# A router's choice by pairwise comparison, two remainders put behind the selection, and one norm's order

## The chip, the cores and the metric

The kernel runs on one core of a Trainium2 chip. The metric is the device time of one execution in microseconds, the median of the runs. A core has five engines that run side by side and meet only at semaphores: TensorE (PE, with PEld for its weight loads), VectorE (DVE), ScalarE (ACT), GpSimd (POOL) and SyncE (SP, which issues most DMAs here).

## The reference, cut to what matters

One inference step of a two-layer decoder over 336 tokens (16 meta tokens, 256 of a prompt, 64 of samples), model width 1024. Layer 0 is RWKV-7 time mixing, layer 1 differential attention; behind each stands the same kind of mixture of 16 experts with a shared router. The change lies in this mixture:

```python
def _moe(x, router_w, router_b, w_gate, w_up, w_down):
    s = jax.nn.sigmoid((xt @ router_w).astype(f32))
    sel = s + router_b.astype(f32)
    grp = lax.top_k(sel.reshape(-1, N_GROUPS, EXPERTS_PER_GROUP), 2)[0].sum(-1)
    _, gidx = lax.top_k(grp, TOPK_GROUPS)                 # 1 of 4 groups
    gmask = jax.nn.one_hot(gidx, N_GROUPS, dtype=f32).sum(1)
    emask = jnp.repeat(gmask, EXPERTS_PER_GROUP, axis=-1) > 0
    _, eidx = lax.top_k(jnp.where(emask, sel, -jnp.inf), TOP_K)   # 2 of its 4 experts
    wts = jnp.take_along_axis(s, eidx, -1)
    wts = wts / wts.sum(-1, keepdims=True)
    gates = ...                                           # wts at the chosen experts
    for e in range(N_EXPERTS):
        h = jax.nn.silu(xt @ w_gate[e]) * (xt @ w_up[e])
        y = y + gates[:, e:e + 1] * (h @ w_down[e])
```

Ahead of it the residual is normalized (`_layernorm(alpha*x + h)`). Ties go to the lower index, as in `top_k`.

## The kernel before

The 336 tokens stand as three tiles of 128, 128 and 80 rows (`TOK`; tile 2 is the one of 80). All instructions are written out by hand, engine by engine, in the order in which they run; each engine works through its own list and waits on semaphores. `experts(l, n0)` is written once per engine and called for each of the two layers. Its routing part runs thus:

- **Norm.** DVE adds the residual out of PSUM and sums each row (`residual`, lines 2187 and 2176), ACT makes the squares and the root (`spread_of`), DVE takes the reciprocal (2195) and scales (2202, `normalize`). PE turns the tile (`turn`, 1253), ACT and DVE copy the turned halves out, PE makes the logits, and ACT the sigmoid. Meanwhile ACT keeps a rounded copy of each normalized tile (`xtm_hi`, `normed_copy`), and what the rounding left, `xtm_lo`, is a subtraction: by POOL for tile 0 and by DVE (`remainder`, 2292) for tiles 2 and 1.
- **Choice.** DVE adds the bias (2334), takes the six pair sums of each group and their maximum (2338, 2340), and then `first_best` three times: maximum, equal, times a weight that falls with the index, maximum, equal. Once it is for the group, twice for the experts within the masked group. A `dve.drain()` stands between steps that depend on each other. The running counts over the tiles follow (2373 to 2376).
- **Rank.** PE multiplies the choice by a triangle of ones and adds the counts: each token's place in its expert's list (semaphore `rt_pe`). Meanwhile DVE makes the weights of the chosen experts (2377 to 2387). Then DVE adds the rank (2391) and `select` (2239) writes the 0/1 matrix that puts tokens in the 64 slots of each expert.
- **Gather.** PE multiplies the parts `xtm_hi`, `xtm_lo` of the three tiles by that matrix, four passes `i` of 12 matmuls. Passes 0 and 2 use PSUM bank 0, passes 1 and 3 bank 1. ACT empties bank 0 and DVE bank 1 (`gathered`, 2245); passes 2 and 3 wait for that. With all four emptied, the expert pairs begin (`pair`): gate, up, down, two experts at a time, eight pairs.

The experts' weights stream through a ring of slots; SP issues the next load when PE has freed a slot (`free`). So the first pair's gate matmuls also start the stream of the later weights.

Of the kernel before, what the change touches and what calls it, by code (L numbers as in the profile page):

```python
# [8 lines left out]
ALU = mybir.AluOpType  # L9
ACT = mybir.ActivationFunctionType  # L10
AX = mybir.AxisListType.X
# [5 lines left out]
P = 128  # L17
# [22 lines left out]
QUAD = 4 * SLOTS  # L40
TURNS = [(0, 1), (2, 3), (4, 5), (6,), (7,)]
ROWS = [0, 1, 0, 1, 0, 1, 0, 0]
ALPHA = 4.0 ** 0.25
# [45 lines left out]
def constants():  # L89
# [26 lines left out]
    parts["iota"] = np.tile(np.arange(CAP), (P, 1))  # L116
    parts["w16"] = np.tile(np.arange(E_, 0, -1), (P, 1))
    parts["w4"] = np.tile(np.arange(G_, 0, -1), (P, 1))
    parts["valid"] = np.concatenate([p < n for _, n in TOK], 1)
    parts["caus"] = np.where(q > p, -BIG, 0.0)  # L120
# [19 lines left out]
def build(nc, I, O, const, at):  # L140
    ctx = ExitStack()
    with ctx:
        sems = {}

        def S(name):
            name = SHARED.get(name, (name, 0))[0]
            if name not in sems:
                sems[name] = ctx.enter_context(nc.semaphore(name))
            return sems[name]
# [589 lines left out]
        def _(pe):  # L739
# [368 lines left out]

            def gather(q, i):

                for h, t in ((0, 0), (0, 1), (0, 2), (1, 0), (1, 2), (1, 1)):
                    t0, k = TOK[t]
                    if q % 4 == 0 and i == 0 and h and t:
                        pe.wait_ge(S("xtm_lo"), 2 * (q // 4) + (1 if t == 2 else 2))
                    for c in (2 * i, 2 * i + 1):
                        o = QUAD * (c % 2)
                        m = mm(ps[:, i % 2, o:o + QUAD], XTM[h][t][0:k, P * c:P * c + P],
                               SelF[q % 2][0:k, t].rearrange("p e s -> p (e s)"), h == t == 0 and c == 2 * i, h == t == 1 and c == 2 * i + 1)
                m.then_inc(S("xg_mm"), 1)

# [52 lines left out]
            def pair(l, n0, j):  # L1173
# [16 lines left out]
                def more_rows():  # L1190
                    if j < PAIRS - 2:
                        pe.wait_ge(S("sel_ready"), q + 2)
                        for i in (2 * (j % 2), 2 * (j % 2) + 1):
                            pe.wait_ge(S(("xga_ready", "xgb_ready")[i % 2]), 2 * (q + 1) + i // 2)
                            gather(q + 1, i)

# [49 lines left out]
            def experts(l, n0):  # L1246
# [44 lines left out]
                pe.wait_ge(S("sel_ready"), 4 * l + 1)  # L1291
                for i in range(4):
                    if i >= 2:
                        pe.wait_ge(S(("xga_ready", "xgb_ready")[i % 2]), 8 * l + i // 2)
                    gather(4 * l, i)
                for j in range(PAIRS):
# [184 lines left out]
        def _(act):  # L1481
# [245 lines left out]
            def experts(l, n0):  # L1727
                if l == 0:
                    act.wait_ge(S("in_lora"), 16 * 7)
                spread_of(2 * l, 0)  # L1730
                spread_of(2 * l, 1)
                turned_copy(l, 0)
                spread_of(2 * l, 2)
                normed_copy(l, 0)
                turned_copy(l, 1)
                turned_copy(l, 2)
                act.wait_ge(S("rt_pe"), 5 * l + 4)
                act.wait_ge(S("rt_dve"), 6 * l + 1)
                f(rt[0][:, 0:32], ps[:, 6, 0:32], ACT.Sigmoid)
                f(rt[0][0:TOK[2][1], 32:48], ps[0:TOK[2][1], 6, 32:48], ACT.Sigmoid).then_inc(S("s_ready"), 1)  # L1740
                normed_copy(l, 1)
                normed_copy(l, 2)
                for i in (0, 2):
                    gathered(4 * l, i)
                for j in range(PAIRS):
                    if j == PAIRS - 1:
                        act.wait_ge(S("route_ready"), l + 1)
                        overflow(act, l, "act", lambda i, b, n: more_block(l, n), lambda: None, lambda: None)
                    pair(l, j)
# [143 lines left out]
        def _(dve):  # L1893
# [386 lines left out]
            def experts(l, n0):  # L2280
# [30 lines left out]
                residual(l, 0)  # L2311
                residual(l, 1)
                normalize(2 * l, 0)
                residual(l, 2)
                normalize(2 * l, 1)
# [14 lines left out]

                score, sel, a1, a2, oh, msk0, msk, _ = rt
                gm, ga, gb, gc = gs
                m12 = ga[:, 0:12]
                tt(v3(sel), v3(score), rbB.unsqueeze(1).to_broadcast([P, 3, E_]), ALU.add)
                dve.drain()

                for d, o, k in ((1, 0, 3), (2, 3, 2), (3, 5, 1)):
# [3 lines left out]
                dve.drain()  # L2341
                top1 = cntf[:, 0:3]

                def first_best(dst, val, tmp, width, weight):

                    dve.tensor_reduce(top1, v3(val), AX, ALU.max)
                    dve.drain()
                    tt(v3(tmp), v3(val), top1.unsqueeze(2).to_broadcast([P, 3, width]), ALU.is_equal)
                    dve.drain()
                    tt(v3(tmp), v3(tmp), weight.unsqueeze(1).to_broadcast([P, 3, width]), ALU.mult)  # L2350
                    dve.drain()
                    dve.tensor_reduce(top1, v3(tmp), AX, ALU.max)
                    dve.drain()
                    tt(v3(dst), top1.unsqueeze(2).to_broadcast([P, 3, width]),
                       weight.unsqueeze(1).to_broadcast([P, 3, width]), ALU.is_equal)
                    dve.drain()

                first_best(gb, gm, ga, G_, mc("w4"))
                gmask = gb.unsqueeze(2).to_broadcast([P, 12, 4])
                tsc(gc, gb, BIG, -BIG, ALU.mult, ALU.add)  # L2360
                tt(g12(a1), g12(sel), gmask, ALU.mult)
                dve.drain()
                tt(g12(a1), g12(a1), gc.unsqueeze(2).to_broadcast([P, 12, 4]), ALU.add)
                dve.drain()
                first_best(msk0, a1, a2, E_, mc("w16"))
                stt(a1, msk0, -2 * BIG, a1, ALU.mult, ALU.add)
                dve.drain()
                first_best(oh, a1, a2, E_, mc("w16"))
                tt(msk, msk0, oh, ALU.add)
                dve.drain()  # L2370
                tt(v3(msk), v3(msk), mc("valid").unsqueeze(2).to_broadcast([P, 3, E_]), ALU.mult)
                dve.drain()
# [14 lines left out]
                tsc(a2, msk, -1e6, 1e6, ALU.mult, ALU.add)  # L2387
                remainder(2)
                dve.wait_ge(S("rt_pe"), 5 * l + 5)
                dve.drain()  # L2390
                tt(rank3.rearrange("p t n -> p (t n)"), a2, ps[:, 7, 0:48], ALU.add)
                dve.drain()
                select(4 * l)
                dve.tensor_reduce(cntp[:, 0:1], ps[:, 7, 64:80], AX, ALU.max)
                cp(cnt_i[0:1, 0:E_], ps[0:1, 7, 64:80])
                dve.drain()
                cp(cnt_i[0:1, E_:E_ + 1], cntp[0:1, 0:1])
                dve.drain().then_inc(S("route_ready"), 1)
                remainder(1)
                dve.wait_ge(S("route_ready"), l + 1)  # L2400
# [182 lines left out]
```

## Time and profile before

| | |
|---|---|
| runs shown | 1216.82, 1219.72, 1220.41 us, median 1219.72 us |
| profiled execution, its own time | 1218.88 us |
| its span | 1217.2 us |
| busy share of the span | PE 89%, DVE 44%, ACT 29%, POOL 6% |
| chain that ended last, by engine | PE 74%, DVE 12%, DMA 6%, ACT 3%, issue 2% |
| TensorE clock, mean granted | 0.937 of 2.4 GHz |
| DMA | 274 MB, 225 GB/s on average |

The busy shares are averages over stages that differ. The routing of a layer is a short stage between two long ones: PE is idle for parts of it, and the weight stream too. A stage's own rows tell what a change there is worth. The profiled execution lies inside the range of the runs, 0.84 us under their median, so its rows can be set against either.

### The profile page before, as it was taken

Reading aid. Unit: us, or ns where it says so; the run is one execution under the profiler, and the core shown is the slowest. Engines: PE = TensorE matmul, PEld = TensorE weight load, DVE = VectorE, ACT = ScalarE, POOL = GpSimd, SP = SyncE. Lnnn points to the kernel's source line nnn. Section 1 sums busy time; section 2 is a strip of 40 time slices with the busy share of each in tenths; the row PEclk is TensorE's granted clock in tenths of the full one; section 3 lists DMA queues with packets and bytes.
Section 4 is the critical chain, followed back from the end, with each engine's and each line's share of the span. In section 5 each row is a group of like instructions: output and inputs, shape, how many; then the busy total and the mean of one; then the engine's idle time right before and its main releaser. Section 6 shows DMA issues by size and latency. Waiting matters only on the chain.

```text
span 1217.2 us, 23537 instructions
## 1 busy us (share of the span) xinstructions
PE 1081.1 (89%) x10193; PEld 760.0 (62%) x10194; DVE 541.1 (44%) x1068; ACT 358.0 (29%) x720; POOL 70.0 (6%) x101
## 2 busy tenths in 40 slices
PE   4989989899888869999998799999879599999984
PEld 3877978899855644555443699976636444444532
DVE  5856536556566571212122754474444631222215
ACT  3435424443232421111111533473232411111102
POOL 2002100011000000000000112011100000000000
PEclk8989979999997979999999899999989699999997
DMA  9503010011041929999999803464733289999991
GB/s 333 215 10 69 19 47 3 3 38 38 25 154 70 396 95 421 422 422 423 422 423 398 316 1 125 159 234 144 290 139 140 106 348 422 423 423 423 422 401 48
DMA packets 58251, 274.16 MB, mean 225 GB/s; under 512 B 5169, under 2 KB 5690, under 8 KB 34082
## 3 DMA queue, kind: packets, MB, share of 16 engines
q1 hardware_dynamic: 48160, 237.58, 48.6%
q0 software_dynamic: 9360, 34.72, 8.8%
q8 instruction: 83, 1.36, 0.5%
q10 hardware_dynamic: 626, 0.32, 0.1%
q14 instruction: 22, 0.18, 0.0%
HBM read 266.18 MB, written 6.46 MB: 224 GB/s over the span
## 4 chain that ended last, share of the span: by engine, by line
PE 74%; DVE 12%; DMA 6%; ACT 3%; issue 2%; DVEq 1%; SPq 0%; POOLq 0%; ACTq 0%; POOL 0%
PE ps L742 69%; DMA arena<-in_moe_w_up 5%; ACT arena L1484 2%; PE ps L883 1%; PE ps L1373 1%; DVE arena L1924 1%; DMA arena<-in_cache_k 1%; ACT arena L1487 1%; PE ps L1089 1%; PE ps L1205 1%; DVE pwr_lo L1930 0%; PE ps L1253 0%; DVE arena L2024 0%; DMA arena<-in_x_prompt 0%; DVE arena L2483 0%
## 5 line engine op out<-in xcount | busy, mean ns | idle before, releaser
L742 PE MATMUL ps<-arena 64*64 64x64 f32 (+10 forms) x7348 | 625.8, 323 | 61.8 <-DVE arena L2376 15.6
L742 PEld LDWEIGHTS ps<-arena 64*64 64x64 f32 (+4 forms) x7348 | 355.5, 140 | 309.1 <-issue 220.7
L1487 ACT COPY arena<-ps 128x512 f32<-128x512 f32 (+7 forms) x294 | 121.4, 432 | 338.8 <-PE ps L742 182.2
L2267 DVE TENSOR_TENSOR arena<-arena,ps 128x512 f32<-128x512 f32 x16 | 17.4, 1085 | 185.5 <-PE ps L742 185.5
L1484 ACT ACTIVATE arena<-ps,arena 128x256 f32<-128x256 f32 (+5 forms) x96 | 45.5, 507 | 133.5 <-PE ps L742 102.4
L2278 DVE SCALAR_TENSOR_TENSOR yy_lo<-ps,arena,yy_hi 128x512 fp32r<-128x512 f32 x32 | 22.7, 747 | 123.0 <-ACT yy_hi L1484 123.0
L1484 ACT ACTIVATE pw_hi<-arena 128x1024 fp32r<-128x1024 f32 x40 | 42.0, 1057 | 89.0 <-PE ps L742 82.8
L742 PE MATMUL ps<-px_hi,pw_hi 128*128 128x336 f32 x192 | 63.4, 330 | 1.4 <-DVE px_lo L2157 1.0
L742 PE MATMUL ps<-px_lo,pw_hi 128*128 128x336 f32 x192 | 61.9, 322 | 0.0
L742 PE MATMUL ps<-px_hi,pw_lo 128*128 128x336 f32 x192 | 61.8, 322 | 0.0
L1484 ACT ACTIVATE yy_hi<-ps,arena 128x512 fp32r<-128x512 f32 x32 | 20.5, 684 | 106.3 <-PE ps L742 106.3
L1484 ACT ACTIVATE arena<-arena 128x1024 f32<-128x1024 f32 (+9 forms) x73 | 42.9, 629 | 26.9 <-DVE arena L2176 20.6
L2146 DVE TENSOR_TENSOR pw_lo<-arena,pw_hi 128x1024 fp32r<-128x1024 f32 x24 | 29.4, 1225 | 43.2 <-ACT pw_hi L1484 43.1
L742 PE MATMUL ps<-rx_hi_hi,pwr_hi 128*128 128x336 f32 x96 | 34.3, 357 | 12.6 <-ACT rx_hi_hi L1484 8.0
L742 PE MATMUL ps<-yy_hi,sg 128*128 128x512 f32 (+1 forms) x96 | 40.4, 421 | 4.8 <-DVE arena L2256 2.7
L1930 DVE TENSOR_TENSOR pwr_lo<-arena,pwr_hi 128x1024 fp32r<-128x1024 f32 x24 | 29.4, 1223 | 33.8 <-ACT pwr_hi L1484 33.6
L742 PE MATMUL ps<-pw_hi,px_hi 128*128 128x512 f32 (+1 forms) x96 | 40.7, 424 | 4.1 <-ACT pw_hi L1484 3.8
L1484 ACT ACTIVATE arena<-ps 128x512 f32<-128x512 f32 (+4 forms) x23 | 11.4, 506 | 103.9 <-PE ps L742 103.8
L742 PE MATMUL ps<-pw_hi,px_lo 128*128 128x512 f32 (+1 forms) x96 | 39.6, 413 | 0.0
L742 PE MATMUL ps<-pw_lo,px_hi 128*128 128x512 f32 (+1 forms) x96 | 39.3, 409 | 0.0
L742 PEld LDWEIGHTS ps<-px_hi,pw_hi 128*128 128x128 f32 x192 | 37.1, 193 | 1.9 <-issue 1.9
L742 PE MATMUL ps<-yy_lo,sg 128*128 128x512 f32 (+1 forms) x96 | 37.8, 394 | 0.0
(229 smaller groups left out, 1387.3 us busy)
## 6 DMA issues: line engine op xcount, KB each, us to landing
arena<-in_moe_w_gate SPq DMA_DIRECT2D x64, 1024.0 KB, 15.7
arena<-in_moe_w_up SPq DMA_DIRECT2D x64, 1024.0 KB, 18.8
arena<-in_moe_w_down SPq DMA_DIRECT2D x64, 1024.0 KB, 17.0
arena<-in_rwkv_w_rkv SPq DMA_DIRECT2D x6, 2048.0 KB, 19.5
arena<-in_w_kv_shared SPq DMA_DIRECT2D x4, 2048.0 KB, 19.8
arena<-in_cache_k POOLq DMA_DIRECT2D x16, 512.0 KB, 4.6
arena<-in_cache_v POOLq DMA_DIRECT2D x16, 512.0 KB, 6.8
arena<-in_rwkv_w_out SPq DMA_DIRECT2D x2, 2048.0 KB, 10.3
```

What stands on the lines that cost most here:

```text
L742: return pe.matmul(out, lhsT, rhs, start=start, stop=stop)
L883: m = pe.transpose(ps[:, b + hf, P * c:P * c + P], src[:, 4 * hf + c, o0:o0 + P], ident)
L1089: m = pe.transpose(ps[0:n, 4 + g % 4, P * c:P * c + P], X[:, 4 * hf + c, t0:t0 + n], ident)
L1205: m = pe.transpose(ps[:, 2, P * f:P * f + P], HH[:, P * f:P * f + P], ident)
L1373: m = pe.transpose(ps[:, 2 * g + hf, P * c:P * c + P], PGK[b % 4][:, g, P * (4 * hf + c):P * (4 * hf + c) + P], ident)
L1484: return act.activation(out, in_, func, **k)
L1487: return act.copy(out, in_)
L1924: stt(X[:, c, :], sgT[:, c, :], mixv[m][:, c:c + 1], xT[:, c, :], ALU.mult, ALU.add).then_inc(S("mix_ready"), 1)
L1930: tt(lo, w_in(L_RKV + n // 4)[:, :, P * (n % 4):P * (n % 4) + P], hi.bitcast(F32), ALU.subtract).then_inc(S("rw_lo"), 1)
L2146: tt(lo, w_in(L_KV + co // 4)[:, :, P * (co % 4):P * (co % 4) + P], hi.bitcast(F32), ALU.subtract).then_inc(S("pw_lo"), 1)
L2267: tt(HH.rearrange("p (k q) -> p q k", k=NF), HS.rearrange("p (q k) -> p q k", k=NF), bank(3).rearrange("p (q k) -> p q k", k=NF), ALU.mult ...
L2278: stt(YY[ROWS[j]][1][:, h], bank(4 + hf), gsl, YY[ROWS[j]][0][:, h].bitcast(F32), ALU.mult, ALU.subtract).then_inc(S("yl_ready"), 1)
```

## The change

It has three parts, each made in both layers.

1. **The choice.** `first_best` goes. A new function `ahead(val)` takes three tiles of four values, compares every value of a four with every other (`is_gt` and `is_ge`, 48 elements each), puts the `is_ge` result where the other stands first in order (a copy with a mask), and adds up how many stand ahead of each. A group is chosen where nobody stands ahead of it; the four values of the chosen group are summed out of the 16, and `ahead` is run on them. Chosen are those with fewer than 1.5 ahead; rows without a token have the bound -1. Three constants of 23 columns give way to two of 19.
2. **The remainders of tiles 2 and 1** come behind `select`; the counts that `route_ready` announces come behind them. PE's gather is cut to match: passes 0 and 1 first do the parts that need neither remainder, then both do tile 2's, then both tile 1's.
3. **The norm.** `residual` of tile 2 stands ahead of `normalize` of tile 0 on DVE, and ACT makes tile 2's spread ahead of its copy of the turned tile 0.

```diff
+PARTS = [(0, 0), (0, 1), (0, 2), (1, 0), (1, 2), (1, 1)]
-    parts["w16"] = np.tile(np.arange(E_, 0, -1), (P, 1))
-    parts["w4"] = np.tile(np.arange(G_, 0, -1), (P, 1))
-    parts["valid"] = np.concatenate([p < n for _, n in TOK], 1)
+    parts["first"] = np.tile((np.arange(4)[None, :] < np.arange(4)[:, None]).reshape(1, 16), (P, 1))
+    parts["below"] = np.concatenate([np.where(p < n, 1.5, -1.0) for _, n in TOK], 1)
...
-                for i in range(4):
-                    if i >= 2:
-                        pe.wait_ge(S(("xga_ready", "xgb_ready")[i % 2]), 8 * l + i // 2)
-                    gather(4 * l, i)
+                for i in range(2):
+                    gather(4 * l, i, PARTS[0:4])
+                pe.wait_ge(S("xtm_lo"), 2 * l + 1)
+                for i in range(2):
+                    gather(4 * l, i, PARTS[4:5])
+                pe.wait_ge(S("xtm_lo"), 2 * l + 2)
+                for i in range(2):
+                    gather(4 * l, i, PARTS[5:6])
+                for i in range(2, 4):
+                    pe.wait_ge(S(("xga_ready", "xgb_ready")[i % 2]), 8 * l + i // 2)
+                    gather(4 * l, i, PARTS)
...
-                turned_copy(l, 0)
                 spread_of(2 * l, 2)
+                turned_copy(l, 0)
...
-                normalize(2 * l, 0)
                 residual(l, 2)
+                normalize(2 * l, 0)
...
+                def ahead(val):
+                    other = v3(val).unsqueeze(2).to_broadcast([P, 3, 4, 4])
+                    own = v3(val).unsqueeze(3).to_broadcast([P, 3, 4, 4])
+                    tt(g44(r4), other, own, ALU.is_gt)
+                    tt(g44(g4), other, own, ALU.is_ge)
+                    dve.drain()
+                    dve.copy_predicated(v3(r4), mc("first").bitcast(U32).unsqueeze(1).to_broadcast([P, 3, 16]), v3(g4))
+                    dve.drain()
+                    dve.tensor_reduce(ga, g12(r4), AX, ALU.add)
+                    dve.drain()
...
+                ahead(gm)
+                tsc(gb, ga, 0.5, None, ALU.is_lt)
+                dve.drain()
+                tt(g12(a1), g12(sel), gb.unsqueeze(2).to_broadcast([P, 12, 4]), ALU.mult)
+                dve.drain()
+                dve.tensor_reduce(v3(gm), a1.rearrange("p (t g n) -> p t n g", t=3, g=4), AX, ALU.add)
+                dve.drain()
+                ahead(gm)
+                tt(v3(gc), v3(ga), mc("below").unsqueeze(2).to_broadcast([P, 3, 4]), ALU.is_lt)
+                dve.drain()
+                tt(g44(msk), v3(gb).unsqueeze(3).to_broadcast([P, 3, 4, 4]), v3(gc).unsqueeze(2).to_broadcast([P, 3, 4, 4]), ALU.mult)
...
-                remainder(2)
                 dve.wait_ge(S("rt_pe"), 5 * l + 5)
                 ...
                 select(4 * l)
+                remainder(2)
+                remainder(1)
                 ...
                 dve.drain().then_inc(S("route_ready"), 1)
-                remainder(1)
```

On DVE, at the first layer's norm: L2187 and L2176 are `residual`, L2195 and L2202 `normalize`, L2285 the copy of a turned tile. Before, from the reciprocal of tile 0 on:

```order
L2195 RECIPROCAL arena<-arena 128x1 [waits ln_sd]
L2202 TENSOR_SCALAR arena<-arena 128x1024
L2187 SCALAR_TENSOR_TENSOR arena<-arena,ps 80x512 [waits tile_mm]
L2187 SCALAR_TENSOR_TENSOR arena<-arena,ps 80x512
L2176 TENSOR_SCALAR arena<-arena 80x1
L2195 RECIPROCAL arena<-arena 128x1 [waits ln_sd]
L2202 TENSOR_SCALAR arena<-arena 128x1024
L2285 COPY arena<-ps 128x4x128 [waits nt_mm]
```

After, with the same lines six further down (L2193, L2182, L2201, L2208, L2291), from the residual of tile 2 on:

```order
L2193 SCALAR_TENSOR_TENSOR arena<-arena,ps 80x512 [waits tile_mm]
L2193 SCALAR_TENSOR_TENSOR arena<-arena,ps 80x512
L2182 TENSOR_SCALAR arena<-arena 80x1
L2201 RECIPROCAL arena<-arena 128x1 [waits ln_sd]
L2208 TENSOR_SCALAR arena<-arena 128x1024
L2201 RECIPROCAL arena<-arena 128x1 [waits ln_sd]
L2208 TENSOR_SCALAR arena<-arena 128x1024
L2291 COPY arena<-ps 128x4x128 [waits nt_mm]
```

The 80-row residual has moved ahead of the 128-row tile's reciprocal and scaling; the rest keeps its order.

On DVE, from the last step of the weights on: L2391 adds the rank, L2239 is `select`, `xtm_lo_55` and `xtm_lo_54` are the remainders of tiles 2 and 1, L2394 to L2397 the counts, L2245 empties the gather's bank. Before:

```order
L2387 TENSOR_SCALAR arena<-arena 128x48
L2292 TENSOR_TENSOR xtm_lo_55<-arena,xtm_hi_52 80x128x8 [waits xtm_hi]
L2391 TENSOR_TENSOR arena<-arena,ps 128x48 [waits rt_pe]
L2239 TENSOR_TENSOR sel_56<-arena 128x768
L2394 TENSOR_REDUCE arena<-ps 128x1
L2395 CAST cnt_i<-ps 1x16
L2397 CAST cnt_i<-arena 1x1
L2292 TENSOR_TENSOR xtm_lo_54<-arena,xtm_hi_51 128x128x8 [waits xtm_hi]
L2245 TENSOR_SCALAR arena<-ps,arena 128x256 [waits xg_mm,route_ready]
```

After (rank L2392, `select` L2245, remainders L2298, counts L2397 to L2400, emptying L2251):

```order
L2389 TENSOR_SCALAR arena<-arena 128x48
L2392 TENSOR_TENSOR arena<-arena,ps 128x48 [waits rt_pe]
L2245 TENSOR_TENSOR sel_56<-arena 128x768
L2298 TENSOR_TENSOR xtm_lo_55<-arena,xtm_hi_52 80x128x8 [waits xtm_hi]
L2298 TENSOR_TENSOR xtm_lo_54<-arena,xtm_hi_51 128x128x8 [waits xtm_hi]
L2397 TENSOR_REDUCE arena<-ps 128x1
L2398 CAST cnt_i<-ps 1x16
L2400 CAST cnt_i<-arena 1x1
L2251 TENSOR_SCALAR arena<-ps,arena 128x256 [waits xg_mm,route_ready]
```

Both remainders now stand between `select` and the counts, and the wait for `rt_pe` follows straight on the last step of the weights.

On PE, in the second layer's gather (`xtm_hi0`, `xtm_lo0` and so on are the parts of tiles 0 to 2), from the first pass's fourth part on. Before:

```order
L742 MATMUL ps<-sel0_56,xtm_lo0_53 128x256 x2
L742 MATMUL ps<-sel0_56,xtm_lo2_55 128x256 [waits xtm_lo]
L742 MATMUL ps<-sel0_56,xtm_lo2_55 128x256
L742 MATMUL ps<-sel0_56,xtm_lo1_54 128x256 [waits xtm_lo]
L742 MATMUL ps<-sel0_56,xtm_lo1_54 128x256
L742 MATMUL ps<-sel0_56,xtm_hi0_50 128x256 x2
L742 MATMUL ps<-sel0_56,xtm_hi1_51 128x256 x2
L742 MATMUL ps<-sel0_56,xtm_hi2_52 128x256 x2
L742 MATMUL ps<-sel0_56,xtm_lo0_53 128x256 x2
L742 MATMUL ps<-sel0_56,xtm_lo2_55 128x256 x2
L742 MATMUL ps<-sel0_56,xtm_lo1_54 128x256 x2
L742 MATMUL ps<-sel0_56,xtm_hi0_50 128x256 [waits xga_ready]
```

After:

```order
L742 MATMUL ps<-sel0_56,xtm_lo0_53 128x256 x2
L742 MATMUL ps<-sel0_56,xtm_hi0_50 128x256 x2
L742 MATMUL ps<-sel0_56,xtm_hi1_51 128x256 x2
L742 MATMUL ps<-sel0_56,xtm_hi2_52 128x256 x2
L742 MATMUL ps<-sel0_56,xtm_lo0_53 128x256 x2
L742 MATMUL ps<-sel0_56,xtm_lo2_55 128x256 [waits xtm_lo]
L742 MATMUL ps<-sel0_56,xtm_lo2_55 128x256 x3
L742 MATMUL ps<-sel0_56,xtm_lo1_54 128x256 [waits xtm_lo]
L742 MATMUL ps<-sel0_56,xtm_lo1_54 128x256 x3
L742 MATMUL ps<-sel0_56,xtm_hi0_50 128x256 [waits xga_ready]
```

The four matmuls of pass 0 that use the DVE's remainders have moved behind eight of pass 1, and each remainder is now used by both passes in a row; the wait for `xga_ready` (bank 0 emptied) opens pass 2 as before, but fewer matmuls now stand between it and the end of pass 0.

## Rows read from the trace of the kernel before

**Rows 1.** the page: part 4 by line, and one group of part 5
```profile
PE ps L742 69%; DMA arena<-in_moe_w_up 5%; ACT arena L1484 2%; PE ps L883 1%; PE ps L1373 1%; DVE arena L1924 1%; DMA arena<-in_cache_k 1%; ACT arena L1487 1%; PE ps L1089 1%; PE ps L1205 1%; DVE pwr_lo L1930 0%; PE ps L1253 0%; DVE arena L2024 0%; DMA arena<-in_x_prompt 0%; DVE arena L2483 0%
...
L742 PE MATMUL ps<-arena 64*64 64x64 f32 (+10 forms) x7348 | 625.8, 323 | 61.8 <-DVE arena L2376 15.6
```

**Rows 2.** chain of waits, whole program: start us, length us, what
```profile
620.89 29.45 DMA arena<-in_moe_w_up
```

**Rows 3.** windows: stretch, us, busy by engine, PEclk, DMA share, GB/s
```profile
418.00:420.00 2.00, 0.97 (x5) 0.97 (x6) 1.52 (x5) 1.59 (x4) 0.00 (x0) 0.69 1.00 418
430.00:432.00 2.00, 0.00 (x0) 0.00 (x0) 1.45 (x7) 0.00 (x0) 0.00 (x0) 0.50 0.08 33
...
442.00:443.00 1.00, 1.00 (x8) 1.00 (x7) 0.00 (x0) 0.17 (x1) 0.00 (x0) 0.67 0.00 0
```

**Rows 4.** timeline of DVE, first norm: start us, us, line, operation, [idle before]
```profile
415.47 0.16 DVE L2195 RECIPROCAL arena<-arena 128x1 f32<-128x1 f32 x1 [0.23 <-ACT arena L1484]
...
416.44 0.68 DVE L2187 SCALAR_TENSOR_TENSOR arena<-arena,ps 80x512 f32<-80x512 f32 x1
...
417.94 0.15 DVE L2195 RECIPROCAL arena<-arena 128x1 f32<-128x1 f32 x1
```

**Rows 5.** timeline of PE, first routing
```profile
416.58 1.10 PE L1253 MATMUL ps<-arena 128*128 128x128 f32 x8 [1.82 <-DVE arena L2202]
419.03 1.97 PE L1253 MATMUL ps<-arena 128*128 128x128 f32 x8 [1.36 <-DVE arena L2202]
...
433.44 1.46 PE L742 MATMUL ps<-arena 128*128 128x48 f32 x6 [7.79 <-DVE arena L2376]
437.94 1.62 PE L742 MATMUL ps<-sel,xtm_hi 128*128 128x256 f32 x6 [3.04 <-DVE sel L2239]
...
440.91 1.48 PE L742 MATMUL ps<-sel,xtm_hi 128*128 128x256 f32 x6
442.19 1.10 PE L742 MATMUL ps<-sel,xtm_lo 128*128 128x256 f32 x6
443.12 0.88 PE L742 MATMUL ps<-sel,xtm_hi 128*128 128x256 f32 x6
443.84 0.88 PE L742 MATMUL ps<-sel,xtm_lo 128*128 128x256 f32 x6
...
447.30 13.96 PE L742 MATMUL ps<-arena 128*64 128x512 f32 x64 [1.14 <-issue]
```

**Rows 6.** timeline of DVE, choice and selection
```profile
427.02 0.17 DVE L2346 TENSOR_REDUCE arena<-arena 128x3 f32<-128x12 f32 x1
...
428.58 0.17 DVE L2360 TENSOR_SCALAR arena<-arena 128x12 f32<-128x12 f32 x1 [0.41 <-issue]
...
432.60 0.21 DVE L2371 TENSOR_TENSOR arena<-arena 128x48 f32<-128x48 f32 x1
432.88 0.17 DVE L2373 COPY arena<-arena 128x16 f32<-128x16 f32 x1
...
434.35 0.21 DVE L2385 TENSOR_TENSOR arena<-arena 128x48 f32<-128x48 f32 x1
434.48 0.18 DVE L2387 TENSOR_SCALAR arena<-arena 128x48 f32<-128x48 f32 x1
434.57 1.89 DVE L2292 TENSOR_TENSOR xtm_lo<-arena,xtm_hi 80x1024 fp32r<-80x1024 f32 x1
436.56 0.20 DVE L2391 TENSOR_TENSOR arena<-arena,ps 128x48 f32<-128x48 f32 x1
436.84 0.96 DVE L2239 TENSOR_TENSOR sel<-arena 128x768 fp32r<-128x768 f32 x1
...
438.29 1.97 DVE L2292 TENSOR_TENSOR xtm_lo<-arena,xtm_hi 128x1024 fp32r<-128x1024 f32 x1
```

**Rows 7.** timeline of ACT, first gathered copy
```profile
441.15 1.02 ACT L1484 ACTIVATE arena<-ps,arena 128x256 f32<-128x256 f32 x2 [11.63 <-PE ps L742]
```

**Rows 8.** instructions of L2054: ns min/median/max
```profile
L2054 DVE COPY_PREDICATED arena<-arena,ps x50: 429/436/449, 175.5 to 329.7; 128x256 f32<-128x256 uint32 x50
```

More of the change, by code:

```diff
@@ L1107, in key_value_query, with gather @@
                         rows_of(co - 8)
-            def gather(q, i):
-                for h, t in ((0, 0), (0, 1), (0, 2), (1, 0), (1, 2), (1, 1)):
+            def gather(q, i, order):
+                for h, t in order:
                     t0, k = TOK[t]
-                    if q % 4 == 0 and i == 0 and h and t:
-                        pe.wait_ge(S("xtm_lo"), 2 * (q // 4) + (1 if t == 2 else 2))
                     for c in (2 * i, 2 * i + 1):
@@ L1118, in gather @@
                                SelF[q % 2][0:k, t].rearrange("p e s -> p (e s)"), h == t == 0 and c == 2 * i, h == t == 1 and c == 2 * i + 1)
-                m.then_inc(S("xg_mm"), 1)
+                if order[-1] == (1, 1):
+                    m.then_inc(S("xg_mm"), 1)
             def more_block(n0, n):
@@ L1194, in more_rows @@
                             pe.wait_ge(S(("xga_ready", "xgb_ready")[i % 2]), 2 * (q + 1) + i // 2)
-                            gather(q + 1, i)
+                            gather(q + 1, i, PARTS)
                 if j == PAIRS - 1:
@@ L1731, in experts @@
                 spread_of(2 * l, 1)
+                spread_of(2 * l, 2)
                 turned_copy(l, 0)
-                spread_of(2 * l, 2)
                 normed_copy(l, 0)
@@ L2312, in experts @@
                 residual(l, 1)
+                residual(l, 2)
                 normalize(2 * l, 0)
-                residual(l, 2)
                 normalize(2 * l, 1)
@@ L2329, in g12, with g44 @@
                     return x.rearrange("p (g n) -> p g n", n=4)
-                score, sel, a1, a2, oh, msk0, msk, _ = rt
+                def g44(x):
+                    return x.rearrange("p (t i j) -> p t i j", t=3, i=4)
+                score, sel, a1, a2, r4, g4, msk, _ = rt
                 gm, ga, gb, gc = gs
-                m12 = ga[:, 0:12]
+                top1 = cntf[:, 0:3]
+                def ahead(val):
[8 more added lines that the diff above has]
+                    dve.drain()
                 tt(v3(sel), v3(score), rbB.unsqueeze(1).to_broadcast([P, 3, E_]), ALU.add)
@@ L2341, in experts @@
                 dve.drain()
[L2342 to L2361, printed above, removed]
+                ahead(gm)
+                tsc(gb, ga, 0.5, None, ALU.is_lt)
                 dve.drain()
-                tt(g12(a1), g12(a1), gc.unsqueeze(2).to_broadcast([P, 12, 4]), ALU.add)
+                tt(g12(a1), g12(sel), gb.unsqueeze(2).to_broadcast([P, 12, 4]), ALU.mult)
                 dve.drain()
-                first_best(msk0, a1, a2, E_, mc("w16"))
-                stt(a1, msk0, -2 * BIG, a1, ALU.mult, ALU.add)
+                dve.tensor_reduce(v3(gm), a1.rearrange("p (t g n) -> p t n g", t=3, g=4), AX, ALU.add)
                 dve.drain()
-                first_best(oh, a1, a2, E_, mc("w16"))
-                tt(msk, msk0, oh, ALU.add)
+                ahead(gm)
+                tt(v3(gc), v3(ga), mc("below").unsqueeze(2).to_broadcast([P, 3, 4]), ALU.is_lt)
                 dve.drain()
-                tt(v3(msk), v3(msk), mc("valid").unsqueeze(2).to_broadcast([P, 3, E_]), ALU.mult)
+                tt(g44(msk), v3(gb).unsqueeze(3).to_broadcast([P, 3, 4, 4]), v3(gc).unsqueeze(2).to_broadcast([P, 3, 4, 4]), ALU.mult)
                 dve.drain()
```

## The prediction

> **What bounds the kernel now.** I read the chain of waits first. PE carries most of it, and one transfer stands out: the up weights of the last expert pair, 29.45 us [rows 2], and since all such waits make 5% of the 1217.2 us span, some 61 us, there is one like it in each layer [rows 1]. So the end of an expert stage hangs on its weight stream. The stream, though, is idle before: its share is 0.08 in the two microseconds from 430 [rows 3], while DVE makes the choice. It goes on when the first pair's matmuls, from 447.30 on [rows 5], free slots. What the routing saves therefore moves PE's first gate matmul, the stream and the stage's end alike, unless something fails to move along; nothing in these rows is tied to a fixed time.
>
> Then I read the routing on the engines' timelines. PE idles 7.79 us until the choice is made (DVE L2376), again 3.04 us until the selection [rows 5]. The page gives 15.6 us for the first of these waits in both layers together, twice the 7.79 [rows 1]: the second layer repeats the first, so I work out one layer and double it.
>
> **Part 1, the choice.** What goes lies between the group's maximum at 427.02 and the copy at 432.88 [rows 6]: 5.86 us, all of it on the path, since PE waits. In it 0.34 us is a hole: 0.41 idle before L2360 [rows 6], where drained steps leave about 0.07 (0.28 from start to start, 0.21 long, as between 432.60 and 432.88).
> What comes: `ahead` is four instructions on 48 or 12 elements. Two comparisons stand without a drain between, and such a pair starts 0.13 apart (434.35, 434.48) [rows 6]. The second, the masked copy and the sum are drained: 0.28 each. That is 0.97 us, twice 1.94. Five further drained steps (group mask, product, sum over groups, comparison with the bound, product) at 0.28 make 1.40. In all 3.34, and 3.68 with a hole, which I keep because its cause isn't visible. Saved: 5.86 - 3.68 = 2.18 us.
> Not shown at this size is the masked copy. The nearest row, 128x256, has a median of 0.436 us [rows 8]; 48 elements can't need more. Nor less than the 0.17 us of a 12-element step. With 0.07 of drain the price lies between 0.24 and 0.51; I take the 0.28 of a 48-element step, because the operand has that size, and keep -0.08 to +0.46 for the two.
> [...]
>
> **Part 2, the remainders.** Before, DVE's remainder of tile 2 (1.89 us) stands between the weights and the rank; the rank starts at 436.56 [rows 6]. PE has finished the rank's matmuls at 433.44 + 1.46 = 434.90 [rows 5]. Without the remainder the wait for `rt_pe` decides: 434.90 and the 0.10 that lie between the remainder's end (436.46) and the rank, 435.00. Saved: 1.56 us. Behind the waiting instruction stand `select` and both remainders, all later than the PE result anyway.
> The price is paid in the gather. Call its start G; it stays 1.38 us behind the rank (437.94 - 436.56). The remainders now start with the 0.87 us that select holds DVE (436.84 to 437.71, from 0.96 long less an overlap of 0.09, as at 434.48) and end at about G + 1.7 and G + 3.6. PE's pace in the gather is 1.28/6 = 0.213 us per matmul (440.91 to 442.19), later 0.72/6 = 0.12 (443.12 to 443.84) [rows 5]; in between the granted clock goes from the lower level (1.2 GHz) to the upper one (0.67 is the mean of that microsecond) [rows 3], about 4.7 us after G. At the slow pace PE needs tile 2's remainder after 16 matmuls, at G + 3.5, and tile 1's after 20, at G + 4.4: both are ready, the second by 0.8 us.
> But pass 0 now ends with its 22nd matmul instead of its 12th: 22 x 0.213 and 0.14 for the start (1.42 us of the first six less 1.28) give G + 4.83. Only then can ACT empty bank 0: it starts 0.24 after PE's next matmul would (441.15 against 440.91) and takes 1.02 [rows 7], and PE goes on some 0.1 later (the gap between two engines seen at the rank): pass 2 starts at G + 6.19. Before it started at 443.12, G + 5.18; ACT's work lay beside pass 1, and that cover is gone but for two matmuls. Passes 2 and 3 and their emptying are as before. Cost: 1.01 us.
> Bounds: if the level rises early, the gather waits for the remainder of tile 1 instead, two matmuls and the same 1.36 follow, G + 5.0: -0.2. If it rises only after pass 3, 24 matmuls lose 0.093 each: +2.2 on top, 3.2 in all.
>
> **Part 3, the norm.** The residual of tile 2 takes 1.50 us from its first row to the next reciprocal (416.44 to 417.94), so tile 0's reciprocal goes from 415.47 [rows 4] to about 416.66, 1.19 later, for PE's work that produced the residuals is done by then. The first turn on PE, at 416.58 before, starts at 417.77 and with its 1.10 us ends at 418.87 [rows 5]. Tile 1's normalize is ready by about 418.73 and no longer queued behind the residual; the second turn can thus start at 418.87 instead of 419.03. From there PE works without a gap through the logits, so this is the path: -0.16 us. ACT's reordered spread is done when the turned tile 0 arrives, and tile 2's turn is queued behind other PE work anyway. The bound upward: the granted clock fell during the idle time before 419.03 (0.69 in 418 to 420 [rows 3]), and the second turn took 1.97 us where the first took 1.10. If the first falls under the lower level too, it ends at 419.74: +0.71.
>
> **Sum.** -2.18 - 1.56 - 0.16 + 1.01 = -2.89 us a layer, -5.8 us in all. From the profiled execution's own 1218.88 us that gives 1213.1; the median of the runs is 0.84 higher, and for it I forecast **1213.9 us**, 0.5% less. A measurement of this kernel can tell about 0.3%, 3.7 us, from no change (the runs before lie 3.6 us apart).
> All lower bounds together: -2.18 - 0.34 (no hole) - 0.08 - 1.56 - 0.30 - 0.2, the 0.30 being the norm if the second turn starts as soon as tile 1 is ready; -4.7 a layer, 1210.4. All upper ones: -2.18 + 0.46 + 0.34 (a second hole) - 1.56 + 0.71 + 3.2 = +1.0 a layer, 1221.7; these would have to meet, in both layers.
>
> **Rivals**, each from the median.
> *The clock rises early in the gather.* The rank's matmuls now end only 1.5 us before G (434.90 to 436.38 in the old times), where it was 3.04. For it: PE is busier ahead of the gather. Against: idle until the rank is PE's state as before, and before the change PE worked 4.7 us at the lower level. The gather then costs -0.2 instead of 1.01: -4.1 a layer, 1211.5 us.
> *The lower level takes back what the routing saves.* The first turn at the lower level costs 0.87 more than forecast, passes 2 and 3 at it 2.2: together 3.1 against the 2.89 saved, and 1220.1 us. With the gather alone, 1218.3; with the first turn alone, 1215.7. For it: both stages do lie near a change of level [rows 3]. Against: in the gather the level rose before pass 2 although PE came out of idleness.
> *The new hold in the gather makes it slower than before.* PE stands still for 0.9 us (G + 5.26 to G + 6.19) between pass 1 and pass 2. If the clock then falls back at the start of pass 2 and comes back only behind the first 4.7 us of the gate matmuls, passes 2 and 3 lose 2.2 us and the gate matmuls 2.35: -2.89 + 4.55 = +1.7 a layer, 1223.0, and with the upper bound of the masked copy 1224.0. It decides once the fallen clock costs more than the 2.89 us saved. For it: after 1.36 us of idle before 419.03 the second turn ran slow. Against: before 447.30 PE idled 1.14 us [rows 5], and the gate matmuls ran 13.96/64 = 0.218 us for 512 columns, the pace of 0.12 for 256 and not of 0.213.
> The Trainium skill's page "TensorE: Matmul & The Clock Gate", section "A second HAM failure mode: psum-queue depth-cycling", says that a PE idling briefly between groups of matmuls as it cycles through PSUM banks can swing between the levels and lose throughput; this hold is of that kind. The row at 447.30 does not bear it out for one gap.
>
> **How the numbers follow.** The forecast has 0.62, the early clock 0.14, the lower level 0.20 (a quarter of it the first turn alone, still faster by over 0.3%), the slower case 0.04. Faster by over 0.3% (under 1216.1): 0.62 + 0.14 + 0.05 = 0.81, less 0.03 for the spread of the medians, 0.78. Slower by over 0.3% (above 1223.4): 0.04. Within: 0.18. The range runs from 1209.8 (the lower bounds and the spread of the runs) to 1218.0 (just under the lower level in the gather alone).
>
> **What would show it.** Right: PE's wait before L2378 shrinks from 7.79 to about 5.6 us, the one before the gather from 3.04 to about 1.5, a new PE wait of 0.9 us for ACT stands before pass 2, the first gate matmul comes 2.9 us earlier in relation to the end of the output projection, the transfer wait stays at 29 us. Wrong: a masked copy well over 0.28 us, a wait for `xtm_lo` in the gather, a longer first turn, or a transfer wait that grows by what the routing saves.

## The result, and the profile after

The changed kernel took 1210.53 us in the median of six runs, 0.9939 of the kernel before (95% interval 0.9915 to 0.9962). The six runs of before that belong to it have a median of 1216.74 us, 6.2 us more. Timed again beside 30 runs of before (median 1219.47) it was 1211.21 us in 11 runs, ratio 0.9936 (0.9912 to 0.9960): 7.8 us less, between 4.9 and 10.7. Forecast were 5.8 us less and 1213.9 us. The direction was right and the difference lies inside this interval, but the forecast time was some 3 us too high.

The profiled execution has a span of 1205.3 us, 11.9 less than before's. Not all of it is the change's. The table takes a routing apart. A routing here is the stretch from DVE's first residual row to PE's first gate matmul, cut at the starts of rows: norm and logits up to the bias, choice up to the last running count, rank up to the row that adds it, selection up to the first gather matmul, and gather.

| us | norm | choice | rank | selection | gather | sum |
|---|---|---|---|---|---|---|
| before, layer 0 | 13.85 | 7.22 | 3.35 | 1.38 | 9.36 | 35.16 |
| after, layer 0 | 13.66 | 5.02 | 1.80 | 1.38 | 10.43 | 32.29 |
| forecast of the difference | -0.16 | -2.18 | -1.56 | 0 | +1.01 | -2.89 |
| before, layer 1 | 13.94 | 7.20 | 3.34 | 1.38 | 9.44 | 35.30 |
| after, layer 1 | 12.58 | 4.67 | 1.86 | 1.38 | 10.14 | 30.63 |

Layer 0 gave 2.87 us and layer 1 4.67, 7.5 together. The other 4.4 lie in stages with the same code. The first residual row, for instance, stood at 412.14 before and at 409.49 after; in the runs below it came between 406.97 and 412.96, as it chanced.

PE's timeline after, first layer and then second, answers to [rows 5]:

```profile
415.10 2.93 PE L1252 MATMUL ps<-arena 128*128 128x128 f32 x16 [2.99 <-DVE arena L2208]
...
428.40 1.46 PE L742 MATMUL ps<-arena 128*128 128x48 f32 x6 [5.58 <-DVE arena L2378]
431.35 1.62 PE L742 MATMUL ps<-sel,xtm_hi 128*128 128x256 f32 x6 [1.49 <-DVE sel L2245]
...
434.48 2.28 PE L742 MATMUL ps<-sel,xtm_lo 128*128 128x256 f32 x10
437.50 0.98 PE L742 MATMUL ps<-sel,xtm_hi 128*128 128x256 f32 x6 [0.74 <-ACT arena L1490]
...
441.78 4.51 PE L742 MATMUL ps<-arena 128*64 128x512 f32 x20 [1.14 <-issue]
...
936.23 2.06 PE L1252 MATMUL ps<-arena 128*128 128x128 f32 x16 [2.91 <-DVE arena L2208]
```

The wait for the choice is 5.58 us where it was 7.79, the one for the selection 1.49 where it was 3.04, and the hold for ACT is there, 0.74 (0.88 in the second layer). Pass 2 starts 6.15 us behind the gather's start in layer 0, where 6.19 was forecast, and 5.87 in layer 1. The two turns run in one piece now: 2.93 us in layer 0, 2.06 in layer 1. Before, the two layers did not differ here. These are layer 1's turns before, to be set beside 1.10 and 1.97 in layer 0 [rows 5]:

```profile
941.88 1.09 PE L1253 MATMUL ps<-arena 128*128 128x128 f32 x8 [1.69 <-DVE arena L2202]
944.34 1.94 PE L1253 MATMUL ps<-arena 128*128 128x128 f32 x8 [1.37 <-DVE arena L2202]
```

DVE's timeline after, first layer and one row of the second, answers to [rows 6]:

```profile
424.19 0.21 DVE L2348 TENSOR_TENSOR arena<-arena 128x48 f32<-128x48 f32 x1
424.32 0.20 DVE L2349 TENSOR_TENSOR arena<-arena 128x48 f32<-128x48 f32 x1
424.59 0.22 DVE L2351 COPY_PREDICATED arena<-arena 128x48 f32<-128x48 uint32 x1
424.88 0.20 DVE L2353 TENSOR_REDUCE arena<-arena 128x12 f32<-128x48 f32 x1
425.16 0.17 DVE L2364 TENSOR_SCALAR arena<-arena 128x12 f32<-128x12 f32 x1
425.76 0.21 DVE L2366 TENSOR_TENSOR arena<-arena 128x48 f32<-128x48 f32 x1 [0.43 <-issue]
...
429.97 0.20 DVE L2392 TENSOR_TENSOR arena<-arena,ps 128x48 f32<-128x48 f32 x1 [0.35 <-PE ps L742]
430.25 0.96 DVE L2245 TENSOR_TENSOR sel<-arena 128x768 fp32r<-128x768 f32 x1
431.12 3.83 DVE L2298 TENSOR_TENSOR xtm_lo<-arena,xtm_hi 80x1024 fp32r<-80x1024 f32 x2
...
949.09 0.18 DVE L2385 RECIPROCAL arena<-arena 128x3 f32<-128x3 f32 x1 [0.41 <-issue]
```

The masked copy takes 0.22 us, 0.29 to the next start, where 0.28 was taken. The undrained pair starts 0.13 apart. The hole (0.43 us in which DVE waits for nothing that the profile shows) is still in the choice of layer 0. In layer 1 it has slid to the weights of the experts, where the wait for PE's rank hides nearly all of it. The remainders end 3.6 us behind the gather's start.

The chain of waits after, answering to [rows 2]: the transfer wait is still there in both layers, about as long as before (29.45 and 29.02 us). It starts 173.3 and 173.1 us behind the first gate matmul, where it was 173.6 and 173.8. So the stream did move along with that matmul.

```profile
615.06 29.86 DMA arena<-in_moe_w_up
...
1134.39 29.57 DMA arena<-in_moe_w_up
```

### The profile page after: what moved, and what is told of

It is laid out like the page before. It is cut to its first block, busy times and chain, and to the rows that moved or that the text cites. A ratio compares the mean times of both kernels' runs of the same rounds, so it can differ in the third digit from the quotient of the medians.

```text
span 1205.3 us, 23503 instructions
## 1 busy us (share of the span) xinstructions
PE 1076.9 (89%) x10193; PEld 755.7 (63%) x10194; DVE 537.3 (45%) x1052; ACT 358.0 (30%) x720; POOL 70.1 (6%) x101
## 3 DMA queue, kind: packets, MB, share of 16 engines
q8 instruction: 83, 1.36, 0.5%
## 4 chain that ended last, share of the span: by engine, by line
PE 75%; DVE 11%; DMA 6%; ACT 3%; issue 2%; DVEq 1%; SPq 0%; POOLq 0%; ACTq 0%; POOL 0%
PE ps L742 69%; DMA arena<-in_moe_w_up 5%; ACT arena L1490 1%; PE ps L883 1%; PE ps L1379 1%; DVE arena L1930 1%; DMA arena<-in_cache_k 1%; ACT arena L1493 1%; DVE arena L2193 1%; PE ps L1089 1%; PE ps L1204 1%; DVE pwr_lo L1936 0%; DMA arena<-in_x_prompt 0%; DVE arena L2030 0%; PE ps L760 0%
```

## The experiments

The theories A and B, or A and a rival, stand with each run. Each ratio is to the kernel before, timed beside it, with its 95% interval behind it. Lengths are those of the table's columns, layer 0 and layer 1, from one profiled execution of each kernel. "The level" is that of TensorE's granted clock: 1.00 in a window's column PEclk is the upper level (2.4 GHz), 0.50 the lower one (1.2 GHz). Where a text says when the level rose or fell, that is an estimate from the mean of the window in which it did.

**The changed kernel again.** 

> The changed kernel itself, timed again beside the one before. In the profiled execution the two routings (first residual row on DVE to the first gate matmul) went from 35.16 and 35.30 us to 32.29 and 30.63: -7.5 us together; the other 4.4 of the span's 11.9 us lie in stages that the change leaves alone. Theory A (the terms of the sum hold, and only TensorE's level moves a routing by a us or so): the median difference is between -5 and -8 us, and the stages left alone differ in both directions from run to run. Theory B (the change also shortens other stages): about -10 us or more, and the stretch from the start to the first residual is again 2.6 us shorter than before.

Measured: 0.9936, as above. Routings 32.23 and 30.46 us, norm 13.61 and 12.54, all as in the first profile. The 7.8 us lie in A's range, though the interval (4.9 to 10.7) reaches B's. The first residual row stood at 408.44, 3.7 us earlier than before, which is B's sign. But in the next run, with the same code in front, it stood at 412.82. So that stretch varies from profile to profile, and A is the better supported.

**Part 1 alone** (`first_best` replaced by `ahead`, nothing else). 

> Part 1 alone. Theory A: bias to running counts goes from 7.2 us to 4.7-5.0 in each layer and everything behind keeps its length: 32.8 us per routing, about -4.7 us in all. Theory B (a gather that starts earlier meets another level of the clock, as it chances): the choice is as short, but the gather changes by up to 1 us either way, -3 to -7 us.

Measured: 0.9939 (0.9914 to 0.9964), 1212.51 us. Choice 5.03 and 4.68; the routings 32.40 and 32.49, 5.6 us less together, because the gather also fell, to 8.80 and 8.85. In layer 1 the hole has moved into the rank here (3.68 us for 3.34), where nothing hides it. PE's timeline, second layer:

```profile
959.93 1.74 PE L741 MATMUL ps<-sel,xtm_lo 128*128 128x256 f32 x6
961.47 1.19 PE L741 MATMUL ps<-sel,xtm_hi 128*128 128x256 f32 x6
962.49 0.88 PE L741 MATMUL ps<-sel,xtm_lo 128*128 128x256 f32 x6
```

The pace of 0.12 us is there from 962.49 on, with pass 1's second half; before, it held from pass 2 on [rows 5]. So B is right on the gather here: the same gather, started 2.2 us earlier in its routing, met the upper level sooner, some 3.6 us behind its start where before it was 4.7 in layer 0 and 4.9 in layer 1.

**Part 2 alone.** 

> Part 2 alone. Theory A: counts to rank from 3.35 us to 1.8, gather (first matmul to first gate) from 9.4 us to 10.1-10.4 by the hold before pass 2: -0.5 to -0.9 us per routing, -1 to -2 us in all, not to be told from none by the time alone. Rival: the hold is covered and the whole 1.55 us is kept, -3 us.

Measured: 0.9991 (0.9969 to 1.0012): not to be told from none. Rank 1.81 and 1.80, hold 0.87 in both, gather 9.71 and 9.65: 1.2 to 1.3 us less per layer behind the choice. That lies between A and the rival: the hold came, as A said, but the gather grew by only 0.35 and 0.21 us, because the level rose some 3.3 and 3.2 us behind its start. But layer 0's norm took 16.08 us in the profile, 2.2 more than before, in code that this part leaves alone. PE's timeline and two windows there:

```profile
419.90 3.60 PE L743 MATMUL ps<-arena 128*32 128x128 f32 x40
423.86 0.72 PE L743 MATMUL ps<-arena 128*80 128x16 f32 x4 [0.36 <-DVE arena L2305]
```
```profile
420.00:422.00 2.00, 2.00 (x21) 1.58 (x22) 0.78 (x2) 1.20 (x1) 1.51 (x1) 0.50 1.01 410
422.00:424.00 2.00, 1.64 (x21) 1.31 (x22) 0.24 (x1) 0.00 (x0) 0.00 (x0) 0.50 1.00 422
```

The logits ran at the lower level (0.50), 3.60 us where the other profiles, and layer 1 of this one, have 2.09. That a norm can lose 2 us to the level without an edit to its code is in none of the forecast's terms. Whether this is chance or belongs to this kernel, one profile can't tell.

**Part 3 alone.** 

> Part 3 alone. First residual row to bias: 13.85 us and 13.94 before, 13.66 and 12.58 with the change. Theory A (the order of the norm gives 0.2 us; the other 1.2 in the second layer came from TensorE standing at its upper level during the turns, which differs from run to run): 13.7 in a layer where the turns run at the lower level and 12.6 where they run at the upper one, without a fixed place. Rival B (the new order itself gives 1.2 us in the second layer, where the data stand otherwise): 13.7 and 12.6 again. In all -0.3 us by A at the lower level, -1.4 by B.

Measured: 0.9982 (0.9963 to 1.0), norm 13.67 and 12.58; turns of 2.85 and 2.06 us:

```profile
418.57 2.85 PE L1253 MATMUL ps<-arena 128*128 128x128 f32 x16 [2.99 <-DVE arena L2202]
...
943.68 2.06 PE L1253 MATMUL ps<-arena 128*128 128x128 f32 x16 [2.91 <-DVE arena L2202]
```

These are the norms of the whole change too, and all six profiles that have the new order and no added work ahead of the turns agree within 0.06 us (layer 0) and 0.04 (layer 1). So it is not chance; the number is B's. But the routings, 35.08 and 34.68, are only 0.7 us shorter together, not 1.4: layer 1's gather, whose code this part leaves alone, took 10.18 us for 9.44, because the level rose there some 6.6 us behind its start. The windows of the changed kernel show what differs between the layers in the turns:

```profile
415.00:417.00 2.00, 1.91 (x13) 1.80 (x14) 1.68 (x5) 1.91 (x5) 0.00 (x0) 0.77 1.01 422
417.00:419.00 2.00, 2.00 (x22) 1.25 (x20) 1.50 (x2) 1.72 (x2) 0.63 (x1) 0.50 1.01 422
...
936.00:938.00 2.00, 1.77 (x15) 1.67 (x16) 1.69 (x5) 1.86 (x5) 0.00 (x0) 1.00 1.00 422
938.00:940.00 2.00, 1.68 (x31) 1.08 (x32) 1.85 (x6) 2.00 (x3) 0.44 (x1) 1.00 1.02 430
```

In layer 0 the level falls during the turns, in layer 1 it stays up. Before the turns PE stood idle for nearly the same time in both (2.99 and 2.91 us). In layer 0 the level fell 6.5 to 6.7 us behind the first residual row in the old order and the new alike (5.9 in part 2's run); in layer 1, in the old order, it fell at 6.8 to 7.0. The turns of the new order begin 5.6 us behind that row. Why such a small difference keeps the level up in layer 1 is not shown.

**Transposes that keep PE busy ahead of the norm.**

```diff
+                keep(18, 7)      # 18 x pe.transpose(ps[:, 7, 0:P], ident, ident)
                 turn(0)
```

> The changed kernel with 18 more transposes of a constant into an unused PSUM bank, right behind the output projection, where PE stands idle for 3 us until the first turn (18 x 0.137 = 2.5 us at the upper level). Nothing reads them. Theory A (the 1.1 us between the layers, 13.6 against 12.5 from the first residual row to the bias, is TensorE's level during the turns): the level stays up, both layers take 12.5 us, -1.1 us in all. Rival B (layer 0 is longer for another reason, its data or its loads): 13.6 and 12.5 as without, or longer where the added work is in the way.

Measured: 0.9895 (0.9869 to 0.9921), 1208.23 us. Norm 12.58 and 12.56. PE's timeline, layer 0:

```profile
410.64 2.13 PE L1277 MATMUL ps<-arena 128*128 128x128 f32 x18
413.79 2.05 PE L1252 MATMUL ps<-arena 128*128 128x128 f32 x16 [1.02 <-DVE arena L2213]
...
435.11 1.65 PE L742 MATMUL ps<-sel,xtm_hi 128*128 128x256 f32 x6 [0.68 <-ACT arena L1495]
436.56 1.48 PE L742 MATMUL ps<-sel,xtm_lo 128*128 128x256 f32 x6
```

With PE busy ahead of them the turns take 2.05 us in layer 0 too: the 1.1 us between the layers is TensorE's level, as A has it, and the data are not its cause. What the run also shows is the level's price further on: layer 0's gather, now begun 1.1 us sooner in its routing, was still at the lower level when it came to the hold of 0.68 us, ran pass 2 at that level and took 11.94 us; the level rose some 9.6 us behind its start, where it was 5.2 in the changed kernel. So layer 0 of this profile lost 0.4 us by the transposes, 32.73 for 32.29. The median gained 3 us against the 1211.21 of the changed kernel, though the intervals overlap. That the transposes also spare the losses seen in part 2's run fits, but was not shown.

**Four banks for the gather.**

```diff
                 for i in range(2, 4):
-                    pe.wait_ge(S(("xga_ready", "xgb_ready")[i % 2]), 8 * l + i // 2)
-                    gather(4 * l, i, PARTS)
+                    gather(4 * l, i, PARTS, 2 + i)      # PSUM bank 4 or 5
...
```

ACT and DVE empty the same banks to match.

> The changed kernel, with passes 2 and 3 of the gather in PSUM banks 4 and 5 instead of 0 and 1, so that they wait for no emptying. Theory A (the hold before pass 2 is the price of part 2): the 0.74 and 0.88 us of hold go, first gather matmul to first gate falls from 10.4 and 10.0-10.1 us to about 9.6 and 9.3, -1.6 us against the changed kernel. Rival: the level decides, and passes 2 and 3 that start sooner run more of their matmuls at the lower one; then less than 0.5 us per layer is left.

Measured: 0.9907 (0.9876 to 0.9938), 1208.97 us. Gather 9.39 and 8.98, 1.0 and 1.2 less than after. PE's timeline, layer 0:

```profile
434.47 2.28 PE L742 MATMUL ps<-sel,xtm_lo 128*128 128x256 f32 x10
436.58 0.87 PE L742 MATMUL ps<-sel,xtm_hi 128*128 128x256 f32 x6
...
440.74 5.80 PE L742 MATMUL ps<-arena 128*64 128x512 f32 x26 [1.13 <-issue]
```

Pass 2 follows pass 1 without idle time, and the level rose where it did in the changed kernel, some 5.2 and 4.2 us behind the start. So the comparison is clean. Theory A: the hold was part 2's price, and it is gone.

**The passes one after the other**, the remainders still behind the selection. 

> The changed kernel, with passes 0 and 1 one after the other as before the change; the remainders stay behind the selection. Theory A: pass 0 waits for tile 1's remainder, which ends 3.6 us behind the first gather matmul (at 0.213 us a matmul it is wanted at 2.3), ACT's emptying lies beside pass 1 again, pass 2 starts at 3.6 + 2 x 0.21 + 12 x 0.21 = 6.6 us or, with the upper level coming in between, some 6.0: the same 10.2 to 10.6 us of gather, so the cut of the passes gives or takes less than 0.5 us. Rival (the cut is what makes the change pay): 1 us or more slower per layer than the changed kernel.

Measured: 0.9946 (0.9922 to 0.9970), 1214.11 us; gather 11.74 and 11.17, 1.0 to 1.3 us more per layer. A missed, the rival is right. Pass 0 waited 1.03 us for tile 1's remainder, as A said, and the level then rose some 8.6 us behind the first gather matmul in layer 0, not 5.2:

```profile
434.26 0.79 PE L742 MATMUL ps<-sel,xtm_lo 128*128 128x256 f32 x2 [1.03 <-DVE xtm_lo L2296]
...
438.70 1.13 PE L742 MATMUL ps<-sel,xtm_lo 128*128 128x256 f32 x6
```

So the recut of the gather, which the forecast booked only as a cost, saves that wait. The rest of the difference is the later rise. By the median alone the two kernels can't be told apart, since the intervals overlap.

**Transposes ahead of the gather.** 18 ahead of the rank, 5 behind it. 

> The changed kernel with 18 more such transposes in front of the rank's matmuls, where PE is idle for 5.2 to 5.6 us, and 5 between these and the gather (1.5 us idle). Nothing reads them. Theory A (the gather's first 5 us run at the lower level because PE came out of idleness): the level is up when the gather starts, passes 0 and 1 then wait for tile 1's remainder (3.6 us behind the first gather matmul), pass 2 starts at about 5.0 instead of 6.1, -1.1 us per layer, -2.2 in all. Rival (short work does not hold the level): the gather as long as without, and up to 0.5 us later where the five transposes run at the lower level.

Measured: 0.9928 (0.9899 to 0.9958), 1210.88 us, no different from the changed kernel. The transposes ended 3.58 us before the rank, and the gather began at the lower level as before (pass 0's first half 1.42 us, 431.99 to 433.41). So A's gain did not come. It is not a fair test of idleness, since most of it was left. Yet the rank of layer 0 shows that the level outlasted those 3.58 us:

```profile
429.32 0.84 PE L742 MATMUL ps<-arena 128*128 128x48 f32 x6 [3.58 <-DVE arena L2384]
```

In the changed kernel it took 1.46. There the level fell only between the rank and the gather, in spite of the five transposes. In layer 1, after 3.23 us of idle time, it had fallen by the rank (1.41 us).

**Spread transposes, four banks, first parts first.** 

> The changed kernel with four things: passes 2 and 3 in banks 4 and 5; all four passes first do the parts that need no DVE remainder, then each pass its remaining four matmuls; 18 unread transposes behind the output projection; and 27 more, spread over PE's idle time from the logits to the gather (released by the sigmoid and by ACT's two copies, so that they do not end early). Theory A (idleness just ahead of the gather is what puts it at the lower level): the level is up at the gather, 32 matmuls x 0.12 = 3.8 us until the remainders are wanted, then 1.9 and the last emptying: 7 to 7.5 us from first gather matmul to first gate instead of 10.4 and 10.1; a routing takes 27.5 to 28.5 us, 7 us less than the changed kernel in all. Rival (such short work does not raise the level): 9 to 10 us of gather, no better than with the banks alone.

Measured: 0.9918 (0.9890 to 0.9946), 1209.04 us. In layer 0 the granted clock stayed at 1.00 up to 424 us, with the spread transposes, and was 0.50 in 424 to 426, with the rank. The gather began at 0.21 us a matmul, and the level rose some 3.1 and 4.1 us behind its start; gather 8.48 and 8.94. A's 7 to 7.5 us missed. The rival is right that the level was not up at the gather; its 9 to 10 us missed too, since layer 0's gather is 0.9 us shorter than with the banks alone. The two routings, 29.26 and 29.41 us, are together 1.0 us shorter than in the next kernel, but the median is 5 us longer. Its profiled execution was the fastest of the six, so the rows can't say where the others lost; that stays open.

**Four banks and the 18 transposes ahead of the norm.** 

> The changed kernel with passes 2 and 3 in banks 4 and 5 and the 18 unread transposes behind the output projection, nothing else. Theory A (the two gains add up): norm 12.6 us in both layers, no hold; the first layer's gather then starts 1.1 us sooner and finds the level rising later, as in the run with the transposes alone, so 10.5 to 11 us of gather there and 9.0 in the second: -2 us against the changed kernel. Rival (the later rise eats all of it in the first layer): no better than the banks alone.

Measured: 0.9868 (0.9841 to 0.9895), **1203.74 us**, 15 us under the 1218.76 of before in the same runs, and better than the changed kernel (0.9936, 0.9912 to 0.9960). Norm 12.57 in both layers, gather 9.60 and 8.78, routings 30.37 and 29.26. The two gains add up, in layer 0 better than expected: the late rise of the run with the transposes alone did not come back (some 5.6 us behind the gather's start, not 9.6). The rows account for 3.3 of the 7.5 us between the medians of this kernel and the changed one; where the rest lies stays open.

## Why the prediction was right in all its steps but one, and too small in its size

- **What bounds the kernel**: right. The transfer wait stayed at 29 to 30 us and moved with the first gate matmul.
- **The choice**: right, 2.20 us in layer 0 for 2.18. In layer 1 2.53, because the hole of 0.34, kept since its cause wasn't visible, moved out of the choice. That part was luck. The price of the masked copy was right within 0.01.
- **The remainders**: right, 1.55 and 1.48 us for 1.56, and a hold of 0.74 and 0.88 us for 0.9. The gather cost 1.07 and 0.70 for 1.01. In layer 1 it cost less because the level rose sooner, some 4.3 us behind the start. The four-bank run shows that in layer 0 the hold was all of this price (1.04 of 1.07 us). In the run with the old passes the gather is 2.38 and 1.73 us longer than before, more than part 2 gives: without the recut it would not have paid.
- **The rivals**: none of the three came. The level rose before pass 2 in both layers, as the forecast had it, the turns of layer 0 cost what was forecast, and behind the hold passes 2 and 3 ran at 0.12 us a matmul.
- **The norm**: right in layer 0 (0.19 us for 0.16), wrong in layer 1 (1.36). This is the step that failed. The term of -0.16 kept the second turn at the lower level, where the rows of before have it, and moved only its start. In layer 1 the new order kept the level up: both turns took 2.06 us at a granted clock of 1.00. Part 3 alone shows the same 12.58 us, and the run with transposes ahead of the turns brings layer 0 there too. The clock was weighed as a danger to the turns (a first turn at the lower level, +0.71) and not as a gain, though [rows 3] and [rows 5] showed the second turn slow: the bound of 0.30 below the norm was too tight.
- **The sum**: "the second layer repeats the first, so I work out one layer and double it" carried that term into layer 1. The 15.6 us behind it say only that the two waits for the choice are equal. Yet the rows of layer 1 before (turns of 1.09 and 1.94 us) would not have warned: the layers came apart only with the change. Layer 1 saved 4.67 us where 2.89 were forecast. Of the missing 1.78 us, 1.20 are the norm, 0.35 the choice with its hole and 0.31 the gather, less 0.08 at the rank; layer 0 was forecast within 0.02.
- **The time**: the three runs' median that the forecast started from, 1219.72, was a fair one (30 runs: 1219.47; the six beside the changed kernel: 1216.74). The rows explain 1.8 of the 3 us by which the time was too high. The rest lies within the spread of the medians.

## What to carry to other kernels

A term that is worked out where the clock is near a change of level needs two prices, the loss if the level falls and the gain if it stays up; doubling it for a second, equal-looking stage doubles the assumption too. Moving work off the path of a chain is paid where it lands, and the bill can often be met with a buffer: here two PSUM banks bought the hold back. When single executions differ by several microseconds, read an edit's worth from the rows of its own stage, and the total from many runs.

## What the runs showed of the hardware

The two levels of TensorE's clock were worth as much here as some of the edits. The same turns took 2.06 or 2.93 us, the same logits 2.09 or 3.60, and the gather as it was before between 8.80 and 10.18 us when only its start moved (parts 1 and 3 alone). Eighteen transposes that nobody reads, 2.13 us of PE's idle time, made the turns of layer 0 0.9 us shorter; 27 spread ones ahead of the gather held the level up to 424 us in layer 0 but did not bring the gather's first half to it. Behind 18 in one piece the level outlasted 3.58 us of idle time in layer 0, but not 3.23 us in layer 1. And the hole of 0.35 us in DVE's stream, with no wait in it, stayed in each layer's routing but changed its place with the program: whether it costs anything depends on where it falls.
